# VectorE's one-hot tiles built for eight tokens at a time, in a transformer layer with expert retrieval on one Trainium2 core

## The reference

```python
s = jnp.einsum('nhpd,hpkd->nhpk', q, sub_keys)          # 8 heads, 2 halves, 128 keys
sv, si = lax.top_k(s, 16)
cand = sv[:, :, 0, :, None] + sv[:, :, 1, None, :]
cidx = si[:, :, 0, :, None] * 128 + si[:, :, 1, None, :]
tv, tsel = lax.top_k(cand.reshape(n, 8, 256), 16)
eidx = take_along_axis(cidx, tsel)                      # 8 x 16 = 128 experts per token, of 128 x 128
g = softmax(tv)                                         # 128 gates per token
act = gelu(einsum('nd,ned->ne', xt, u[it])) * g
y = einsum('ne,ned->nd', act, v[it])
```

## Time and profile before

| | |
|---|---|
| median of 3 runs | 2512.48 us (2509.66 to 2512.87) |
| span of the profiled execution | 2510.2 us |
| TensorE busy | 2369.3 us |
| VectorE busy | 1651.6 us |
| ScalarE busy | 870.4 us |
| GpSimd busy | 413.0 us |
| ohA tiles on GpSimd | 288, 235.9 us |
| ohB and ohL tiles on VectorE | 288 + 288, 111.8 + 96.5 us |

### The profile page before, as it was taken

One profiled execution on the slowest core, in us unless ns is written; L12 is line 12 of the kernel. 1 busy time (PEld: TensorE's weight loads), 2 busy tenths in 40 slices (PEclk: granted clock), 3 DMA queues, 4 the chain that ended last, 5 costly groups with the idle time before them and its releaser, 6 DMA issues.

```text
span 2510.2 us, 45012 instructions
## 1 busy us (share of the span) xinstructions
PE 2369.3 (94%) x17147; PEld 2304.7 (92%) x17147; DVE 1651.6 (66%) x2899; ACT 870.4 (35%) x805; POOL 413.0 (16%) x469
## 2 busy tenths in 40 slices
PE   7998787987999999999999999999999999999997
PEld 6998655986999999999999999999999999999996
DVE  5599964555449999978888644455555655655554
ACT  4332234333333333333343333343333333333332
POOL 2108500214000000028878300000000000000000
PEclk9999866997999999999999999999999999999998
DMA  6444300441345444546666655566555665556541
GB/s 252 156 151 138 109 17 34 167 151 68 135 143 172 162 173 172 172 166 219 205 209 203 211 186 191 178 257 237 211 197 198 220 225 205 199 196 240 205 167 55
DMA packets 99139, 436.18 MB, mean 174 GB/s; under 512 B 7264, under 2 KB 44272, under 8 KB 54160
## 3 DMA queue, kind: packets, MB, share of 16 engines
q1 hardware_dynamic: 56304, 393.46, 44.9%
q10 hardware_dynamic: 41760, 37.75, 4.5%
q0 software_dynamic: 1024, 4.30, 0.5%
HBM read 393.56 MB, written 41.93 MB: 173 GB/s over the span
## 4 chain that ended last, share of the span: by engine, by line
PE 72%; DVE 18%; issue 6%; ACT 2%; DVEq 1%; POOL 1%; DMA 0%; ACTq 0%; SPq 0%; POOLq 0%
PE acc L1036 22%; PE acc L1038 22%; PE acc L1037 22%; DVE wl L635 5%; DVE cacc L703 2%; PE mis L1231 1%; PE mis L1232 1%; DVE tsel L910 1%; DVE top L908 1%; PE mis L1131 1%; DVE i L895 1%; DVEq L86 1%; PE mis L1202 1%; DVE cand L913 0%; POOL sqb L1272 0%
## 5 line engine op out<-in xcount | busy, mean ns | idle before, releaser
L387 ACT ACTIVATE wh<-raw 128x2048 fp32r<-128x2048 f32 x331 | 634.0, 1915 | 1215.8 <-PE acc L1038 1210.8
L635 DVE TENSOR_TENSOR wl<-raw,wh 128x2048 fp32r<-128x2048 f32 x331 | 762.1, 2302 | 320.7 <-ACT wh L387 320.4
L1036 PE MATMUL acc<-xh,wh 128*128 128x288 f32 x3008 | 899.8, 299 | 55.9 <-DVE wl L635 45.2
L1037 PE MATMUL acc<-xl,wh 128*128 128x288 f32 x3008 | 889.7, 296 | 0.0
L1038 PE MATMUL acc<-xh,wl 128*128 128x288 f32 x3008 | 886.9, 295 | 0.0
L1036 PEld LDWEIGHTS acc<-xh,wh 128*128 128x128 f32 x3008 | 566.2, 188 | 68.7 <-DVE wl L635 55.1
L1036 PE MATMUL acc<-ah,wh 128*128 128x288 f32 x2048 | 606.3, 296 | 0.4 <-DVE wl L635 0.4
L1037 PE MATMUL acc<-al,wh 128*128 128x288 f32 x2048 | 604.2, 295 | 0.0
L1038 PE MATMUL acc<-ah,wl 128*128 128x288 f32 x2048 | 602.1, 294 | 0.0
L1038 PEld LDWEIGHTS acc<-xh,wl 128*128 128x128 f32 x3008 | 568.6, 189 | 0.0
L1037 PEld LDWEIGHTS acc<-xl,wh 128*128 128x128 f32 x3008 | 567.3, 189 | 0.1
(11 more groups left out here) (201 smaller groups left out, 1792.0 us busy)
## 6 DMA issues: line engine op xcount, KB each, us to landing
raw<-in_u SPq DMA_DIRECT2D x128, 1024.0 KB, 4.9
raw<-in_v SPq DMA_DIRECT2D x128, 1024.0 KB, 4.9
raw<-in_w_mix SPq DMA_DIRECT2D x28, 1024.0 KB, 4.8
h<-hbg ACTq DMA_DIRECT2D x32, 576.0 KB, 2.8
G<-gbuf ACTq DMA_DIRECT2D x18, 1024.0 KB, 5.7
hin<-h SPq DMA_DIRECT2D x32, 576.0 KB, 5.2
gin<-G SPq DMA_DIRECT2D x16, 1152.0 KB, 8.2
raw<-in_w_out SPq DMA_DIRECT2D x16, 1024.0 KB, 4.8
```

Of the source, the lines that this page charges most:

```text
L387: act.activation(wh[:, n % 2], raw[:, n % 4], ACT.Copy).then_inc(hi_done, 1)
L635: dve.tensor_tensor(wl[:, n % 2], raw[:, n % 4], wh[:, n % 2].bitcast(F32), ALU.subtract).then_inc(lo_done, 1)
L1036: pe.matmul(out, wh[:, wr, b, :], mh(j), start=(j == 0), stop=False)
L1037: pe.matmul(out, wh[:, wr, b, :], ml(j), start=False, stop=False)
```

## The change

VectorE no longer makes sixteen tiles in a slot, each with one instruction that compares iota with the token's key number and multiplies by the gate's half. It makes one comparison for the slot's eight tokens into a new float32 tile `eqo` (128 x 8 x 128), with iota repeated over the tokens and the key numbers repeated over the columns. Behind it, once that is complete, two multiplications follow, one for each block, in which the four tokens' comparison is repeated over the two halves and the gates' halves over the columns. `ohB` and `ohL` become one tile `ohBL` (block, half, token, column), beside `ghl`. A wait for the slot's own multiplications is added behind the evacuation, so that the next comparison may write `eqo`. The matmuls are the same, GpSimd's and ScalarE's code too.

```diff
                 ghl = sb(o, "ghl", [P, 2, N], F32R)
-                ohL = sb(o, "ohL", [P, 2, 4, P], F32R)
+                ohBL = sb(o, "ohBL", [P, 2, 2, 4, P], F32R)
+                eqo = sb(o, "eqo", [P, 8, P])
...
-            ohA, ohB = sb(u, "ohA", [P, 2, 4, P], F32R), sb(u, "ohB", [P, 2, 4, P], F32R)
+            ohA = sb(u, "ohA", [P, 2, 4, P], F32R)
...
             def one_hots(gi, s):
 
+                tok = 32 * gi + 8 * s
+                own.done(dve.tensor_tensor(eqo[:], bcast(iota, 8, 1), bcast(gijT[:, 2, ds(tok, 8)], P, 2), ALU.is_equal))
+                own.wait(0)
                 for b in range(2):
                     n = 2 * s + b
                     dve.wait_ge(g_done, 8 * gi + n + 1)
-                    for t in range(4):
-                        tok = 32 * gi + 4 * n + t
-                        for part in range(2):
-                            last = dve.tensor_scalar((ohB, ohL)[part][:, b, t, :], iota, gijT[:, 2, ds(tok, 1)],
-                                                     ghl[:, part, ds(tok, 1)].bitcast(F32), ALU.is_equal, ALU.mult)
-                    last.then_inc(oneB, 1)
+                    dve.tensor_tensor(ohBL[:, b], bcast(eqo[:, 4 * b:4 * b + 4, :], 2, 1),
+                                      bcast(ghl[:, :, ds(tok + 4 * b, 4)].bitcast(F32), P, 3), ALU.mult).then_inc(oneB, 1)
...
-            with dve.Fori(0, U2_ITERS) as i:
+            with dve.Fori(0, U2_ITERS) as i, own.loop(i, 0, U2_ITERS, 4):
                 for s in range(4):
                     lo_next(U0 + 4 * U2_0, i, s)
                     one_hots(i, s)
                     u_evac(i + U2_0, s)
+                    dve.wait_ge(oneB, 8 * i + 2 * s + 2)
...
-                            pe.matmul(mis[:, b, P * t:P * t + P], ohA[:, b, t, :], ohB[:, b, t, :], start=True, stop=False)
-                            ins = pe.matmul(mis[:, b, P * t:P * t + P], ohA[:, b, t, :], ohL[:, b, t, :], start=False, stop=True)
+                            pe.matmul(mis[:, b, P * t:P * t + P], ohA[:, b, t, :], ohBL[:, b, 0, t, :], start=True, stop=False)
+                            ins = pe.matmul(mis[:, b, P * t:P * t + P], ohA[:, b, t, :], ohBL[:, b, 1, t, :], start=False, stop=True)
```

## The result

The changed kernel takes 2592.3 us (2590.5 to 2596.4), 3.3% more than before: the ratio is 1.0328, with a 95% interval of 1.0313 to 1.0342. The direction was forecast, the size was not: 80 us instead of 24, and outside the range. The profiled execution has a span of 2590.1 us, 79.9 more than before's 2510.2.

The account below looks back on a forecast made before the run. TensorE bounds the kernel before, GpSimd the one-hot stage after: 26.9 + 4 x 1.95 = 34.7 us, with 0.85 of waiting 35.55 a trip, 2.6 more; nine trips add 23.6 to 2512.5, giving 2536 us, range 2510 to 2558.

Parts of the forecast that it names:

- The rival of no new hold: One-hot stage: broadcast operands may not hold GpSimd, or it slips through; TensorE stays the bound, 2512 us; chance 15%.
- first term: the holds: One-hot stage: VectorE's three new instructions hold GpSimd's tiles, 0.65 us each, 1.95 us a slot.
- in a back-to-back run the two engines take turns: One-hot slot: GpSimd gets in once between two VectorE instructions, then is held by the next; 0.65 us per new instruction.
- one row of the convolution: Beside VectorE's cacc, GpSimd's tensor_tensor took 0.92 us instead of 0.767; read as the engines taking turns.
- the carried-through example: One slot followed tile by tile: GpSimd's last tile ends at 1308.16 instead of 1306.21, 1.95 us later.
- second term: the waits used up: One-hot trip: of GpSimd's 6.0 us waiting for TensorE, only one block's 0.85 us can't go.
- TensorE's clock should not move: One-hot stage: clock stays at 1.00, as in the stage before, which had waits and was 92.6% busy.
- The rival that GpSimd is shut out: One-hot stage: VectorE's next instruction always wins, GpSimd waits the whole run, 14.5 us a trip, 2596 us; chance 4%.

Follow-up runs that it names:

- The pair without the copy: Gapped kernel and changed kernel, each with GpSimd's token-number copy removed and its loop written out: 2536.8 us and 2565.4 us.
- six matmuls more: Changed kernel plus six unread TensorE matmuls ahead of the wait for each slot's second block: 2559.9 us, ratio 1.0188.
- gaps and no copy: Changed kernel with VectorE waiting at each seam, GpSimd's token-number copy removed and its loop written out: 2536.8 us, ratio 1.0098.
- the kernel with gaps: Changed kernel plus two VectorE waits, giving a real gap between all four instructions that read two SBUF tiles: 2591.6 us, ratio 1.0316.
- the run of four: Changed kernel, comparison made once before the trips, plus an unread third multiplication, so wl and three multiplications run back-to-back: 2592.7 us, single run.
- the one without the copy: Changed kernel, GpSimd's token-number copy removed and its loop written out, nothing else: 2565.4 us, ratio 1.0208.

## Why the prediction was wrong

**Right:** that TensorE is the bound and VectorE's time is worth nothing; the new instructions' 1.22 us (1222 ns); that instructions with two SBUF inputs hold GpSimd, broadcast or not, and that this turns a saving of VectorE into a loss; that GpSimd becomes the bound; that TensorE would wait for ohA in most slots (35 times). The rival of no new hold fell with 94.8 us more for the same tiles.

**Wrong, first term: the holds.** The step that failed is "in a back-to-back run the two engines take turns". It was read from one row of the convolution, whose instructions have another form; between two tensor_tensor instructions GpSimd is passed over at every second seam. A slot like that of the carried-through example costs 3.06 us instead of 1.95. Over all slots GpSimd's tiles and copies take 338.2 us instead of 240.1, 98 us more where 36 x 1.95 = 70 was forecast: 28 us of the error. The pair without the copy bears on this step: with a real gap at each seam 2536.8 us, without 2565.4. But of these 28.6 us only 19 are GpSimd's tiles (324.7 us, against 343.9), and 5 its waits for TensorE (0.6, against 5.8), with a clock of 1.00 against 0.95; the other 4 or 5 lie ahead of the first tile, which began at 1107.0 us in the one and at 1111.5 in the other. Nor do turns cost 0.65 us each: a tile let in took 1.33 us where VectorE had no gap, 0.75 more than undisturbed, and 0.8 to 0.9 more with gaps.

**Wrong, second term: the waits used up.** Of GpSimd's 6.0 us of waiting in a trip, 0.85 should have been left, 7.7 us in nine trips. In fact 34.2 us are left, 23.0 + 11.2, and this is the other 27 us. The forecast added up GpSimd's time and took for granted that a waiting engine loses its waits first. But both engines wait for each other. At the head of a trip GpSimd's copy waits for TensorE, 11.2 us in all; the other 23.0 us stand behind the stretches in which TensorE worked at half speed. Where the clock stayed up, with six matmuls more or with gaps and no copy, this second part was 0 and 0.6 us.

**Wrong, third: the clock.** "TensorE's clock should not move" rested on a stage at 92.6% busy with a clock of 1.00. That stage doesn't carry over: seven waits of up to 1.6 us between 1000 and 1100 us left its clock alone (the line gives us in total, times, longest), while most falls here stand behind waits of 1.1 to 1.2 us.

```profile
PE acc L1036 <- DVE wl L635: 7.4, 7, 1.6
```

With TensorE kept at work the clock stayed at 1.00 and 32 us came back, with not one instruction of GpSimd or VectorE changed. So the second and third term are in the main one and the same: the clock's falls draw GpSimd's waits. That order is read from timelines; the six matmuls remove falls and waits at once, and so does taking the copy away in the kernel with gaps, so no run sets one without the other. What makes one wait bring the clock down and another not stays open: the length of the wait alone doesn't decide it.

The first two terms together give 70 + 28 - 46.4 + 26.5 = 78 us, which is what the stage grew by (98.1 us more work less 19.8 us of waiting). The kernel with gaps and no copy takes 2536.8 us, which is the forecast's 2536, but that is partly luck: GpSimd's work grew by 84.6 us (324.7, against 240.1), not by 70, and its waits fell to 0.6 us, not to 7.7.

**The rival that GpSimd is shut out** had a time near the measured one, 2596 us, for reasons that are half right. It counted 14.5 us of holds a trip, which measured 98.1 / 9 = 10.9, and it left the waits at 0.85 us a trip, which measured 3.8. Its chance of 4% was too small, as one row stood for the turns against it.

## What to carry to other kernels

Before a run of VectorE instructions is fused, look at what GpSimd does at that time: many tensor_scalar instructions left it alone here, three tensor_tensor instructions in each slot, with two SBUF inputs, cost it 98 us, and one input in PSUM took all of it away. A slack of two engines that wait for each other isn't a sum to be spent: look for the place in the trip where a late tile of one makes the other late. And an engine that was the bound and begins to wait can lose its clock, so a load above the slack can cost more than the part by which it exceeds the slack: here 98 us of work against 54 us of waiting, 44 us over, and 80 us lost.

## What the runs showed of the hardware

- A GpSimd tile that reads SBUF ended 0.4 us behind the tensor_tensor that held it. In a run of such instructions, each issued 0.08 us before the last one's end, it got in at every second seam (3.6 and 2.4 us in the run of four), at any seam with a real gap of 0.14 to 0.23 us (1.4 to 1.5 us), and ahead of a scalar_tensor_tensor even without a gap (2.58, then 1.33 us).
- VectorE reads one input of 1024 elements from PSUM as fast as from SBUF: 1217 and 1218 ns, against 1222.
- A wait of VectorE for its own last instruction cost 0.23 us in this loop; in straight code it was 0.03.
- TensorE's granted clock fell behind waits of 1.1 to 1.2 us in the changed kernel (ten times, for 34 us, with none longer than 1.2 us in the one without the copy), and stayed at 1.00 with 34 waits of 0.64 us on average, none over 1.3, in the kernel with gaps and no copy.
- 216 matmuls more made the changed kernel 32 us faster (2592.3 to 2559.9), and the kernel before 26.5 us slower.
